# Experts' token rows moved by indirect DMAs in place of one-hot matmuls

## The reference, cut to what matters

```
logits = x @ w_router                       # 264 x 8
top_val, top_idx = top_k(logits, 2)
gates = softmax(top_val)
for e in range(8):
    y += gate[:, e] * ((silu(x @ Wg[e]) * (x @ Wu[e])) @ Wd[e])      # 1024 -> 3584 -> 1024
x = layer_norm(ALPHA * x + y)
```

## Time and profile before

| | |
|---|---|
| median of the runs | 2019.44 us (2013.46 to 2019.93, three runs) |
| span of the profiled execution | 2015.7 us |
| TensorE busy, clock | 1872.3 us, mean granted clock 0.924 |
| VectorE, ScalarE, GpSimd busy | 1279.3, 966.8, 77.8 us |
| HBM read, written | 446.60 MB, 5.94 MB |

### The profile page before, as it was taken

One profiled execution on the slowest core, in us unless ns is written; L12 is line 12 of the kernel. 1 busy time (PEld: TensorE's weight loads), 2 busy tenths in 40 slices (PEclk: granted clock), 3 DMA queues, 4 the chain that ended last, 5 costly groups with the idle time before them and its releaser, 6 DMA issues.

```text
span 2015.7 us, 24769 instructions
## 1 busy us (share of the span) xinstructions
PE 1872.3 (93%) x9498; PEld 1569.5 (78%) x9499; DVE 1279.3 (63%) x1193; ACT 966.8 (48%) x846; POOL 77.8 (4%) x88
## 2 busy tenths in 40 slices
PE   7999896699999889779999999999999999999994
PEld 6867676599999567667878878878878788788883
DVE  3371555356565131258869868788698687787886
ACT  1431112233332231137757757667577576676672
POOL 3000421000000000000000000000000000000000
PEclk9996778899999996869989999999999998998997
DMA  8540020355554440228969969889799799797990
GB/s 280 189 151 30 1 64 8 104 190 186 186 172 145 146 144 0 100 84 317 373 235 363 373 234 367 307 306 377 273 341 369 241 368 346 253 361 288 326 376 23
DMA packets 209189, 453.40 MB, mean 225 GB/s; under 512 B 6960, under 2 KB 37835, under 8 KB 209075
## 3 DMA queue, kind: packets, MB, share of 16 engines
q1 hardware_dynamic: 203488, 432.12, 60.2%
q0 software_dynamic: 4800, 18.10, 2.8%
q10 hardware_dynamic: 830, 2.21, 0.3%
HBM read 446.60 MB, written 5.94 MB: 225 GB/s over the span
## 4 chain that ended last, share of the span: by engine, by line
PE 71%; DVE 6%; issue 3%; ACT 3%; DVEq 0%; ACTq 0%
PE ps L1584 68%; DVE split_w L1020 2%; DVE sb L1020 2%; PE ps L1581 2%; ACT split_w L947 1%; DVE sb L1266 1%; ACT sb L875 0%; PE ps L1732 0%; DVE sb L1291 0%; ACT sb L974 0%; DVE sb L1554 0%; DVE sel L1453 0%; DVE split_xt L1020 0%; ACT sb L799 0%; DVE sb L1562 0%
## 5 line engine op out<-in xcount | busy, mean ns | idle before, releaser
L1020 DVE TENSOR_TENSOR split_w<-half_slots,split_w 128x2048 fp32r<-128x2048 f32 x378 | 859.7, 2289 | 265.3 <-ACT split_w L947 184.9
L947 ACT ACTIVATE split_w<-half_slots 128x2048 fp32r<-128x2048 f32 x336 | 642.1, 1918 | 195.7 <-PE ps L1584 195.6
L1584 PE MATMUL ps<-split_w,split_xe 128*128 128x512 f32 x2688 | 641.2, 394 | 14.2 <-DVE split_w L1020 12.1
L1584 PEld LDWEIGHTS ps<-split_w,split_xe 128*128 128x128 f32 x2688 | 499.9, 188 | 126.9 <-DVE split_w L1020 21.9
L1584 PE MATMUL ps<-sb 128*128 128x264 f32 (+11 forms) x2180 | 466.4, 375 | 52.1 <-DVEq L1268 10.6
L1584 PEld LDWEIGHTS ps<-sb 128*128 128x128 f32 (+4 forms) x2180 | 378.5, 218 | 137.4 <-issue 54.6
L1584 PE MATMUL ps<-split_w,split_he 128*128 128x512 f32 x1344 | 329.4, 402 | 1.8 <-DVE split_he L1020 1.8
L1584 PEld LDWEIGHTS ps<-split_w,split_he 128*128 128x128 f32 x1344 | 261.0, 195 | 60.2 <-DVE split_he L1020 2.1
L1584 PE MATMUL ps<-x_hi,split_w 128*128 128x264 f32 x896 | 164.9, 286 | 13.4 <-DVE split_w L1020 13.4
L1584 PEld LDWEIGHTS ps<-x_hi,split_w 128*128 128x128 f32 x896 | 140.2, 191 | 13.8 <-DVE split_w L1020 13.8
L1020 DVE TENSOR_TENSOR sb<-sb,ps 128x512 f32<-128x512 f32 (+3 forms) x199 | 117.6, 610 | 50.9 <-PE ps L1584 46.0
(11 more groups left out here) (211 smaller groups left out, 743.0 us busy)
## 6 DMA issues: line engine op xcount, KB each, us to landing
half_slots<-in_moe_w_gu SPq DMA_DIRECT2D x224, 1024.0 KB, 7.3
half_slots<-in_moe_w_down SPq DMA_DIRECT2D x112, 1024.0 KB, 6.8
half_slots<-in_ffn_w_gu SPq DMA_DIRECT2D x28, 1024.0 KB, 5.1
half_slots<-in_ffn_w_down SPq DMA_DIRECT2D x14, 1024.0 KB, 5.0
sb<-in_a_w_in SPq DMA_DIRECT2D x6, 2048.0 KB, 15.1
sb<-in_w_out SPq DMA_DIRECT2D x4, 2048.0 KB, 8.5
sb<-in_b_w_in SPq DMA_DIRECT2D x3, 2048.0 KB, 9.1
sb<-in_cache_mem_v POOLq DMA_DIRECT2D x2, 2048.0 KB, 19.0
```

The costliest lines, as they stand in the source:

```text
L947: act.activation(split_w[:, u % SPLITS, 0, :], halves[half], ACT.Copy).then_inc(sig("unit_hi"), 1)
L1020: return dve.tensor_tensor(o, x0, x1, op)
L1584: return pe.matmul(o, l, r, start=start, stop=stop)
```

## The change

The gather becomes an indirect DMA, and the scatter an adding one:
- ScalarE copies the token rows from PSUM into `x1rows` and stores them in a table in HBM, `x1_rows` (264 x 1024). GpSimd scales them by ALPHA and stores them in a second table, `acc_rows`, of 264 + 128 rows.
- During the routing the eight selections are made one after the other, and three small matmuls for each (`slots`) give, for every slot, the token's number, whether the slot is used, and its gates. From them come the lists `idx_from` and `idx_to` (unused slots point to one of the 128 spare rows) and `gate_sl`.
- GpSimd fetches the 128 rows of expert e+1 with one indirect DMA into `xg` when expert e's rows have been transposed. `rows_T` on TensorE turns them with eight transposes; it stands before unit 38 of the expert ahead, where the gather stood before unit 40. The last hidden slice is transposed before unit 39; it was before unit 40.
- ScalarE scales an expert's result into `yrows` (`y_rows`), and GpSimd adds it into `acc_rows` with one accumulating indirect DMA, waits for it, and frees `yrows`.
- After the last one SyncE loads the three blocks of `acc_rows` back, and the statistics follow.
- The three first units are split before the norm of layer 1 instead of behind the routing. The scatter with zeros before the first expert is gone. The old one-hot path stays for experts with more than 128 tokens.

```diff
@@ SyncE, behind the last weights
+            sp.wait_ge(sig("y_scattered"), 16 * NE)
+            for tt in range(3):
+                n = P if tt < TT else NS
+                sp.dma_start(acc[0:n, tt, :], acc_dram[tt * P:tt * P + n, :]).then_inc(sig(f"acc{tt}_landed"), 16)
@@ GpSimd, at its end
+            def fetch(e):
+                pool.indirect_dma_start(xg, None, x1_dram, bass.IndirectOffsetOnAxis(ap=idx_from[:, e:e + 1], axis=0)).then_inc(sig("xg_landed"), 16)
+
+            pool.wait_ge(sig("idx_ready"), 1)
+            pool.wait_ge(sig("x1_out"), 16 * 3)
+            fetch(0)
+            pool.wait_ge(sig("x1_rows"), 3)
+            for tt in range(3):
+                n = P if tt < TT else NS
+                step(pool.tensor_scalar(acc[0:n, tt, :], x1rows[0:n, tt, :], ALPHA, None, ALU.mult))
+                pool.dma_start(acc_dram[tt * P:tt * P + n, :], acc[0:n, tt, :]).then_inc(sig("acc_out"), 16)
+            pool.dma_start(acc_dram[NT:NT + P, :], acc[:, 0, :]).then_inc(sig("acc_out"), 16)
+            pool.wait_ge(sig("acc_out"), 16 * 4)
+            pool.wait_ge(sig("idx_ready"), 2)
+            pool.sem_inc(sig("yrows_free"), 1)
+            for e in range(NE):
+                if e + 1 < NE:
+                    pool.wait_ge(sig("gathered"), 2 * (e + 1))
+                    fetch(e + 1)
+                pool.wait_ge(sig("y_evicted"), e + 2)
+                pool.indirect_dma_start(acc_dram, bass.IndirectOffsetOnAxis(ap=idx_to[:, e:e + 1], axis=0), yrows, None,
+                                        compute_op=ALU.add).then_inc(sig("y_scattered"), 16)
+                pool.wait_ge(sig("y_scattered"), 16 * (e + 1))
+                pool.sem_inc(sig("yrows_free"), 1)
@@ ScalarE, around the routing
+            act.wait_ge(sig("attn1_lent_back"), 1)
+            for u in range(SPLITS):
+                unit_hi(None, u)
             norm(1, 0, LN_PARTS[1, 0])
...
+            for tt in range(3):
+                n = P if tt < TT else NS
+                halves_of = [("x1tok", 2 * tt + kg) if tt < TT else ("x1tokS", kg) for kg in range(2)]
+                for kg, name in enumerate(halves_of):
+                    free(act.activation(x1rows[0:n, tt, 512 * kg:512 * kg + 512], take(act, *name)[0:n, :], ACT.Copy), *name)
...
+                act.dma_start(x1_dram[tt * P:tt * P + n, :], x1rows[0:n, tt, :]).then_inc(sig("x1_out"), 16)
@@ ScalarE, in the experts
+            def y_rows(t, e):
+                act.wait_ge(sig("units_used"), t * UNITS + 2 * UNITS)
+                act.wait_ge(sig("yrows_free"), t + 1)
+                act.activation(yrows.rearrange("p (a b) -> p a b", a=2), ps[:, 6:8, :], ACT.Copy, scale=gate_sl[:, bass.ds(e, 1)]).then_inc(sig("y_evicted"), 1)
...
+                    if u == UNITS - 1:
+                        if following:
+                            gathered_hi(t + 1)
+                        hidden_T(t, NG - 1)
                     unit_hi(t, u)
-                hidden_T(t, NG - 1)
...
             with act.Fori(0, NE - 1) as e:
-                expert(e)
-                unit_hi(e + 1, 0)
-                gathered_hi(e + 1)
-                unit_hi(e + 1, 1)
-                y_hi(e)
-                unit_hi(e + 1, 2)
+                expert(e, True)
+                for u in range(SPLITS):
+                    unit_hi(e + 1, u)
+                y_rows(e, e)
@@ VectorE, routing (its experts change as ScalarE's do, and lose select, selection_T, y_lo, add_y)
-                dve.tensor_scalar(acc[:, tt, cols], src, ALPHA, None, ALU.mult)
-                free(tt_(split_xt[:, tt, 1, cols], src, split_xt[:, tt, 0, cols].bitcast(F32), ALU.subtract), "x1tok", n)
...
+            select(0, 0, sels[:, 0])
+            select(1, 0, sels[:, 1])
+            tab = [take(dve, "slots", 0), None]
+            step(dve.tensor_copy(idx_from[:, 0:1], tab[0][:, NE:NE + 1]))
+            dve.sem_inc(sig("idx_ready"), 1)
+            free(dve.tensor_copy(slot_tab[:, 0, :], tab[0][:, 0:NE + 2]), "slots", 0)
+            for e in range(2, NE):
+                if e > 2:
+                    dve.wait_ge(sig("slots_read"), e - 2)
+                select(e, 0, sels[:, e % 2])
@@ TensorE
+            for e in range(NE):
+                pe.wait_ge(sig("selected"), e + 1)
...
+                for tt in range(3):
+                    m = P if tt < TT else NS
+                    ins = mm(o[:, c0:c0 + NE + 2], sels[0:m, e % 2, tt, :].bitcast(F32), token_cols[0:m, tt, :], tt == 0, tt == TT)
...
+            def rows_T(t):
+                pe.wait_ge(sig("xg_landed"), t * 16 + 16)
+                for n in range(2):
+                    for q in range(4):
+                        ins = tr(ps[:, 1 + 2 * n, q * P:(q + 1) * P], xg[:, (4 * n + q) * P:(4 * n + q + 1) * P])
+                    ins.then_inc(sig("gathered"), 1)
...
-            def expert(t, before, following):
+            def expert(t, following, direct):
...
-                    if kind == "down" and i == 0 and c == NG - 1:
-                        transpose_h(t, c)
-                        if following:
-                            gather(t + 1)
+                    elif u == ORDER.index(("down", 0, 0)):
+                        pe.wait_ge(sig("y_evicted"), t + 1)
+                    if (kind, c, i) == ("down", NG - 2, 0) and following:
+                        rows_T(t + 1)
+                    if (kind, c, i) == ("down", NG - 2, 1):
+                        transpose_h(t, NG - 1)
```

More of the change, by code:

```diff
@@ L207, in plan_banks @@
     add(("rank",), 1)
+    add(("slots", 0), 0)
+    add(("slots", 1), 6)
     return banks.of
@@ L931, in _ @@
             act.wait_ge(sig("sgu_out"), 16)
[L932 to L936, removed]
+            for tt in range(3):
[3 more added lines that the diff above has]
+                    free(act.activation(x1rows[0:n, tt, 512 * kg:512 * kg + 512], take(act, *name)[0:n, :], ACT.Copy), *name)
+                for name in halves_of:
+                    b, before = bank_of[name]
+                    act.wait_ge(bank_free[b], before + 1)
+                act.sem_inc(sig("x1_rows"), 1)
+                act.dma_start(x1_dram[tt * P:tt * P + n, :], x1rows[0:n, tt, :]).then_inc(sig("x1_out"), 16)
             act.wait_ge(sig("top_diff"), 1)
             act.activation(dtop, dtop, ACT.Exp).then_inc(sig("top_exp"), 1)
[L941 to L947, removed]
             def hidden_T(t, c):
@@ L1397, in _ @@
             dve.sem_inc(sig("sel_ready"), 1)
-            for n in range(2 * TT):
-                tt, kg = divmod(n, 2)
-                src = take(dve, "x1tok", n)
-                cols = slice(512 * kg, 512 * kg + 512)
-                dve.wait_ge(sig("rows_hi"), n + 1)
-                dve.tensor_scalar(acc[:, tt, cols], src, ALPHA, None, ALU.mult)
-                free(tt_(split_xt[:, tt, 1, cols], src, split_xt[:, tt, 0, cols].bitcast(F32), ALU.subtract), "x1tok", n)
-            for n in range(2):
-                cols = slice(512 * n, 512 * n + 512)
-                dve.wait_ge(sig("rows_hi"), 2 * TT + n + 1)
-                free(tt_(split_xt[0:NS, TT, 1, cols], take(dve, "x1tokS", n)[0:NS, :], split_xt[0:NS, TT, 0, cols].bitcast(F32), ALU.subtract), "x1tokS", n)
-            step(dve.tensor_scalar(acc_s, xT[:, :, SEQ:NT], ALPHA, None, ALU.mult))
             dve.wait_ge(sig("top_exp"), 1)
@@ L2042, in scatter @@
                 pe.wait_ge(sig("y_split"), t1 + 1)
-                for k in range(KT):
+                for half in range(2):
                     for part in range(2):
-                        ins = mm(ps[:, 3, k * NS:(k + 1) * NS], split_y[:, part, k * P:(k + 1) * P], selT[:, SEQ:NT], part == 0, part == 1)
+                        ins = mm(ps[0:NS, 1 + 2 * half, :], selT[:, SEQ:NT], split_y[:, part, 512 * half:512 * half + 512], part == 0, part == 1)
                 ins.then_inc(sig("scattered"), 1)
@@ L2099, in expert @@
                     if kind == "gate" and i == 1 and c:
-                        if c == 1:
+                        if c == 1 and not direct:
                             pe.wait_ge(sig("summed"), t * 3 + 5)
                         transpose_h(t, c - 1)
-            gather(0)
+            rows_T(0)
             with pe.Fori(0, NE - 1) as e:
                 expert(e, True, True)
-            expert(NE - 1, True, False)
-            scatter(NE)
+            expert(NE - 1, False, True)
             runs = pe.value_load(turn[0:1, 2 * NE:2 * NE + 1], min_val=NE, max_val=3 * NE)
```

203 lines of the change are left out of this document (118 added, 85 removed).

## The result

The kernel after takes 1883.43 us (median of four runs, 1879.6 to 1885.63), the kernel before on the same chip 2017.37 (four runs, 2013.46 to 2019.93). The ratio is 0.9339, 95% interval 0.9322 to 0.9355. The profiled execution of after has a span of 1883.9 us, 131.8 less than the 2015.7 of before. A second profile of the same program, taken in the experiments, has 1876.6, and their difference of 7.3 us lies wholly ahead of the routing: the logits start at 860.41 in one and at 852.65 in the other. So intervals inside one trace are compared here, and what lies ahead of the logits is left out.

What follows compares the result with a forecast made beforehand. TensorE's own matmul work and the few waits around it were taken as the bound. Head 885, experts 966.0 and tail 31.1 gave a span of 1882.1 us, with a 3.7 us surplus 1886 us, range 1868 to 1898.

Steps and rivals of the forecast that it cites:

- The pace: Time of one expert: 117.5 steady, 0.8 transposes, 1.9 waits, 0.4 for DMA, so 120.6 us against 137.06.
- The term of the waits: TensorE's waits at an expert's seam: 0.4 at its end, 0.7 at unit 3, 0.74 at unit 5; 1.9 us.
- today's 0.74 us stays: At unit 5, the second table load and the Silu still come before it, so the 0.74 us wait remains.
- The price of a fallen clock: At the seam, if the clock fell as in the kernel before, 2.15 us an expert would come back.
- The DMA: Fetch and adding store beside the weights: 4.9 us of engine time an expert, mostly hidden by the lead, 0.4 us charged.
- The head: Up to the first weight matmul: at 885 us, between 882 and 890, instead of 892.81; 7.8 us won.
- The tail: After the last weight matmul: eviction 1.1, adding store 7, reload 4.3; 33.2 us become 31.1.
- The sum: Whole span: 885 + 966.0 + 31.1 = 1882.1 us, 133.6 less than before; 1886 us with a 3.7 surplus.
- A bound by DMA: Rival, in the experts: DMA bandwidth sets the pace, 1897 to 1999 us, taken as 1905; 0.22 together with the clock rival.
- A clock that still falls: Rival, in the experts: the clock drops as before, 15 us more, 1901 us; 0.22 together with the DMA bound.
- Slow ends: Rival, at head and tail: indirect DMAs cost 5 us in the head, 11.3 in the tail; 1902 us; chance 0.10.
- Slower by a store that holds the engines: Rival, in the experts: the adding store blocks the 16 DMA engines; at 30 us, pace 148 and 2105 us; chance 0.05.

Runs made afterwards that it cites:

- narrow back: Kernel after plus 48 matmuls of 128 columns, results thrown away, where the removed gather stood, seven times; 1957.47 us.
- wide back: Kernel after plus 38 matmuls of 512 columns, results thrown away, ahead of the transposes of the next expert's fetched rows, seven times; 1941.34 us.
- scatter back: Kernel after plus 16 matmuls of 8 columns, 8 of 512 and 6 small ones ahead of unit 2 of every expert, results thrown away; 1920.14 us.
- no store: Kernel after with the accumulating store left out for experts 0 to 6, the last one kept; 1881.29 us.
- three stores: Kernel after with every expert's result stored with the add three times, one behind the other; 1897.87 us.
- rows first: Kernel after with the first expert's rows transposed after four slot tables, the fifth behind them, three inside the first expert; 1872.93 us.

## Why the prediction was right, and where it wasn't

- **The pace**, 120.6 forecast, 119.95 measured. The steady part and the transposes (0.8; 0.79 measured) came as worked out. The clock stayed at 1.00, and narrow and wide back show that the reason given for it was the right one. The term of the waits, 1.9, was a little large. The pace has 1.65 above 117.5 + 0.8: some 0.4 at unit 40 as forecast, 0.41 at unit 3 for 0.7, some 0.2 at unit 5 for 0.74, and the rest in small gaps that the forecast had no term for. The step "today's 0.74 us stays" at unit 5 was wrong: that wait belonged to the scatter ahead of it, as scatter back shows. The price of a fallen clock was too low: 2.15 us an expert counted only the matmuls behind the gather, and by the estimate above some 5 of narrow back's 11.0 are the clock's.
- **The DMA**, 0.4 us an expert forecast, nothing measured for the stores. The engine time of 4.9 us was a fair guess: the queue shows 4.0. The smallest leads of experts 1 to 7 lie between 1.1 and 4.1 us, where 5.3 were worked out as spare. That a used-up lead turns into lost time was not right: even three stores cost 0.5 us an expert. The price from below, "it fits into gaps", was the right end. The share of 358 GB/s that the prediction took from the Trainium skill and weighed was passed all through, with 376. The Trainium skill (HBM Reference, Specifications (TRN2)) has a core that streams alone well above that share, about 425, and the trace's figure is above the share too.
- **The first weight matmuls**, 2.0 us for the low clock, came as said in the main: the first expert takes 121.62 us, 1.65 more than the others.
- **The head**, 7.8 us forecast, 2.7 measured. This is the term that was mis-sized. The offsets of the exponential and of the first selection were right, and the fetch landed in 4.8 us for 5.5; 3.5 us of transposes and splits behind it are 3.54. What failed is "at about 0.9 us each eight end near 881, and the tables behind them near 882". The row that it leans on the earlier trace rows, seven small matmuls recorded as 14 in 1.73 us, 0.12 each, stands where the clock is up: 0.93 in before from 866 to 870. The tables (six records each) run at 0.50, 0.25 us a record: 1.5 us each, to 890.3, and VectorE's selections wait for them; at 1.00, inside the first expert of rows first, one takes 0.75. I had read a duration without its clock. The rows then wait 6.6 us in SBUF, the last 1.0 for VectorE, which copies the tables out of PSUM. Rows first took 6.7 us out of the head. The three unit splits that were moved ahead, at no cost by the forecast, were moved back in no run.
- **The tail**, 31.1 forecast, 29.7 measured: the adding store 6.16 for 7, the reload 3.15 for 4.3.
- **The sum**, 1882.1 us of span, came within 1.8 of the 1883.9 because the errors go against each other: experts and tail 8.0 us better, the head 5.1 worse, the stretch ahead of the logits 4.7 later, which is less than two executions of after differ by there (7.8). That the sum came this close is in part luck. The 3.7 us added on top of the span are no real surplus: they set a median against the span of another execution, and wherever a run's own span is on record, its time is 1.7 to 1.9 us more.
- **The rivals.** A bound by DMA: out, by no store and three stores. A clock that still falls: out, by 1.00 in all seven windows. Slow ends: out, the store landed sooner than the plain row of 8.0 us, the reload than its 3.9. Slower by a store that holds the engines: out; three in a row, some 30 us from the first issue to the last landing, cost 0.5 us an expert.

## What to carry to other kernels

The one-hot gather, narrow matmuls in a stream of wide ones, cost more here than its own time, since the clock of what follows was lost as well: put back, it takes 11.0 us, about half of them the clock's. The scatter put back costs about its own 5 us and keeps the clock at 1.00. The adding store of half a megabyte beside the weights cost nothing, and three in a row cost little though they used up the lead of the loads: the waits of the next engine in the chain, ScalarE's for TensorE, gave way first. At the ends of the program, where nothing covers it, count the adding store at its landing (6 us here) and look at what else queues between landing and use. Before judging an edit of 5 us by medians, compare the same interval inside the traces, since what lies ahead of the edit can differ by more.

## What the runs showed of the hardware that was not expected

- A run of 48 matmuls of 128 columns loses the full clock although the profile shows TensorE busy in every microsecond of it: 1.00 up to 1137, 0.50 from 1138 to 1146. The Trainium skill (TensorE: Matmul & The Clock Gate, Part 1: The HAM clock gate) ties the lower level to an idle engine; by that narrow back would have cost 61 us at most, it cost 77.
- The add makes a store by index half again to twice as long (6.1 to 6.8 us for 3.3 to 4.1, alone), and all forms take 3 to 6 us longer beside the weights.
- The same program's start of the logits lay at 852.65 us in one execution and at 860.41 in another. The difference builds up in steps within the first 300 us, and the traces show the granted clock going with them. The first 101 matmuls of both have it at 0.94 in the one and 0.83 in the other, and take 27.9 and 30.6 us; 202 matmuls from 120.44 and from 123.15 on have 0.86 and 0.77, and take 45.9 and 50.6 us. Why the clock differs stays open, since no run was made for it.
